# Sparse-attention weights scaled on GpSimd, values with v stationary, three branches summed in two PSUM banks

## The reference, cut to what matters

```
p_c = masked_softmax(q·kc - slope·dist)      # 15 compressed keys
o_c = p_c · vc
p_s = masked_softmax(q·ks - slope·dist)      # selected blocks: with 256 tokens all of them
o_s = p_s · vs
p_w = masked_softmax(q·kw - slope·dist)      # window of 512: the causal triangle
o_w = p_w · vw
masked_softmax: e = exp(s - max(s)); e / max(sum(e), 1e-30)
out = g0 * o_c + g1 * o_s + g2 * o_w         # g = sigmoid(gate_logits)
```

## Time and profile before

| | |
|---|---|
| median of 3 runs | 2322.37 us (2321.93 to 2323.93) |
| the profiled execution | 2321.79 us, span 2320.1 us |
| mean granted TensorE clock | 0.996 |
| TensorE busy | 2297.4 us, 99%, 13730 matmuls |
| VectorE busy | 1510.8 us, 65% |
| ScalarE busy | 1220.3 us, 53% |
| GpSimd busy | 63.2 us, 3%, 110 instructions |
| HBM read | 402.97 MB, 175 GB/s |

### The profile page before, as it was taken

How to read it: one execution, slowest core, us unless ns; L and a number is a source line. 1 busy time by engine, 2 the same in 40 slices (tenths; PEclk the granted TensorE clock), 3 DMA queues, 4 the chain that set the end, 5 groups by cost and what they waited for, 6 DMA issues and landing times.

```text
span 2320.1 us, 33059 instructions
## 1 busy us (share of the span) xinstructions
PE 2297.4 (99%) x13730; PEld 2003.9 (86%) x13730; DVE 1510.8 (65%) x2004; ACT 1220.3 (53%) x1813; POOL 63.2 (3%) x110
## 2 busy tenths in 40 slices
PE   8999999999999999999999999999999999999998
PEld 7888999988888889999888888888888988788887
DVE  5567656565665676565656765686777765785766
ACT  6555445464564554454545545454655554455554
POOL 0000000000000000000000100000000100000000
PEclk9999999999999999999999999999999999999999
DMA  8564543445545645434555434444555444445553
GB/s 287 189 212 181 204 146 128 167 179 190 192 175 188 212 180 204 146 128 166 214 191 191 164 145 153 151 151 163 208 182 182 164 146 164 145 163 181 183 189 109
DMA packets 61085, 406.69 MB, mean 175 GB/s; under 512 B 7784, under 2 KB 9320, under 8 KB 13576
## 3 DMA queue, kind: packets, MB, share of 16 engines
q1 hardware_dynamic: 60936, 404.58, 49.1%
HBM read 402.97 MB, written 2.10 MB: 175 GB/s over the span
## 4 chain that ended last, share of the span: by engine, by line
PE 94%; DVE 3%; ACT 2%; issue 1%; DMA 0%; SPq 0%; POOL 0%; DVEq 0%; POOLq 0%; ACTq 0%
PE bank L533 20%; PE bank L535 19%; PE bank L534 19%; PE bank L580 18%; PE bank L581 9%; DVE w_lo L249 1%; PE bank L1798 1%; PE bank L1658 1%; PE bank L2204 1%; PE bank L2230 0%; PE bank L396 0%; PE bank L2397 0%; PE bank L1961 0%; PE bank L1981 0%; PE bank L1971 0%
## 5 line engine op out<-in xcount | busy, mean ns | idle before, releaser
L249 DVE TENSOR_TENSOR w_lo<-w_raw,w_hi 128x2048 fp32r<-128x2048 f32 x368 | 837.9, 2284 | 84.0 <-ACT w_hi L241 83.7
L241 ACT ACTIVATE w_hi<-w_raw 128x2048 fp32r<-128x2048 f32 x368 | 702.3, 1911 | 126.3 <-DMA w_raw<-in_tiles 126.0
L580 PE MATMUL bank<-hT,w_hi 128*128 128x512 f32 x1920 | 680.6, 398 | 0.6 <-DVE w_lo L249 0.6
L581 PE MATMUL bank<-hT,w_lo 128*128 128x256 f32 x1920 | 539.0, 281 | 0.0
L580 PEld LDWEIGHTS bank<-hT,w_hi 128*128 128x128 f32 x1920 | 360.7, 188 | 89.6 <-DVE w_lo L249 1.4
L581 PEld LDWEIGHTS bank<-hT,w_lo 128*128 128x128 f32 x1920 | 362.6, 189 | 2.0
L533 PE MATMUL bank<-hT,w_hi 128*128 128x256 f32 x976 | 283.8, 291 | 0.0
L533 PE MATMUL bank<-w_hi,hT 128*128 128x512 f32 (+2 forms) x768 | 273.8, 357 | 5.6 <-DVE hT L385 5.6
L534 PE MATMUL bank<-hT,w_hi 128*128 128x256 f32 x976 | 278.1, 285 | 0.0
L535 PE MATMUL bank<-hT,w_lo 128*128 128x256 f32 x976 | 277.9, 285 | 0.0
L534 PE MATMUL bank<-w_lo,hT 128*128 128x512 f32 (+2 forms) x768 | 269.3, 351 | 0.0
(11 more groups left out here) (376 smaller groups left out, 3021.4 us busy)
## 6 DMA issues: line engine op xcount, KB each, us to landing
w_raw<-in_tiles SPq DMA_DIRECT2D x368, 1024.0 KB, 4.8
a_cmp_w<-in_cmp_w SPq DMA_DIRECT2D x2, 2048.0 KB, 7.7
w_raw<-in_tiles SPq DMA_DIRECT2D x8, 256.0 KB, 5.7
a_gm_rows<-in_rows SPq DMA_DIRECT2D x2, 768.0 KB, 6.5
x_res<-in_x SPq DMA_DIRECT2D x2, 512.0 KB, 5.8
a_ret_rows<-in_rows SPq DMA_DIRECT2D x2, 512.0 KB, 8.3
b_rows<-in_rows SPq DMA_DIRECT2D x2, 512.0 KB, 6.4
out<-x_res SPq DMA_DIRECT2D x4, 256.0 KB, 2.0
```

Source lines behind the costliest of these rows:

```text
L241: act.activation(k.hi[slot][:], k.raw[slot][:], ACT.Copy).then_inc(k.hi_done[slot], 1)
L249: dve.tensor_tensor(k.lo[slot][:], k.raw[slot][:], k.hi[slot][:].bitcast(F32), ALU.subtract).then_inc(k.lo_done[slot], 1)
L580: pe.matmul(bank[:], k.hi[slot][:, at:at + P], k.hT[:, c].rearrange("p a s -> p (a s)"), start=c == 0, stop=False)
L581: last = pe.matmul(bank[:, SEQ:2 * SEQ], k.lo[slot][:, at:at + P], k.hT_hi[:, c], start=False, stop=c == KC - 1)
```

## The change

1. Compressed attention: VectorE multiplies the weights by gate over sum before the turn (semaphore `scaled`), ahead of its filler work up to `cmp_pT`. `pT` becomes twice as large with zeros in half of it (a GpSimd memset), ScalarE copies into it in two halves of the partitions, and two products with `vd` stationary and 512 columns moving open banks 4 and 5, features in partitions.
2. Selected and window attention: a new `pool` program on GpSimd raises the sum to the power -1, multiplies by 1 + gate, and multiplies the two spans of the weights by it in place. The turn waits for that (`scaled`) instead of for the exponents.
3. Values: v stationary (64 columns), `pT` moving; all items add to what the compressed products left in banks 4 and 5. The heads are taken in the order 0, 5, 1, 4, ..., so that the two of a pair write different halves of the partitions. The values of a pair come an iteration later, behind the next pair's scores.
4. The filler units of an iteration stand together: 3, then 2 in each, then 1 and 3.
5. `weighted`, `y` and the turn of `y` go; ScalarE and VectorE split banks 4 and 5 directly, with the scale 0.5.
6. Grouped-query attention: the values of a pair come an iteration later too; filler units 2, 4, 4, 4, 2.

```diff
@@ Compressed @@
+        pool.wait_ge(self.part_mm, 2)
+        pool.memset(self.pT, 0.0).then_inc(self.pT_zeroed, 1)
...
-        f.vector(dve, "cmp_pT")
         dve.wait_ge(self.pr_ok, 1)
...
-        f.vector(dve, "cmp_pv")
-        for t in range(NT):
-            dve.wait_ge(self.pv_mm, t + 1)
-            last = dve.tensor_tensor(self.y[:, t]..., k.bank[4 + t]..., m[...], ALU.mult)
+        dve.tensor_tensor(self.pr[:], self.pr[:], m[:].unsqueeze(2).broadcast_to(wide), ALU.mult).then_inc(self.scaled, 1)
+        f.vector(dve, "cmp_pT")
...
-        act.activation(self.pT, self.k.bank[2][:], ACT.Copy).then_inc(self.pt_ok, 1)
+        act.wait_ge(self.pT_zeroed, 1)
+        for half in range(2):
+            r = slice(64 * half, 64 * half + 64)
+            last = act.activation(self.pT[r, :, half]..., self.k.bank[2][r, :]..., ACT.Copy)
+        last.then_inc(self.pt_ok, 1)
...
-        pe.wait_ge(self.pr_ok, 1)
+        pe.wait_ge(self.scaled, 1)
...
-        for a in range(4):
-            last = pe.matmul(k.bank[4 + a // 2][...], self.pT[:, a * P:(a + 1) * P], self.vd[:, a % 2, :], start=True, stop=True)
+        for g in range(2):
+            pe.matmul(k.bank[4 + g][:], self.vd[:, g], self.pT[:, g].rearrange("p f s -> p (f s)"), start=True, stop=False)
@@ Attention @@
-PAIRED = (0, 4, 1, 5, 2, 6, 3, 7)
+PAIRED = (0, 5, 1, 4, 2, 7, 3, 6)
...
         def turn_p(u):
-            pe.wait_ge(self.pr_ok, u + 1)
+            pe.wait_ge(self.scaled, u + 1)
...
+        def pv(p):
+            pe.wait_ge(self.pt_ok, 2 * p + 2)
+            for kc in range(2):
+                for u in (2 * p, 2 * p + 1):
+                    h, br = PAIRED[u % NSA_H], u // NSA_H
+                    d, c = P * br + 64 * (h // 4), h // 2
+                    out = k.bank[4 + c // 2][64 * (h % 2):64 * (h % 2) + 64, (c % 2) * SEQ + kc * P:(c % 2 + 1) * SEQ]
+                    keys = pT[u % 2][:, SEQ:SPAN] if kc else pT[u % 2][:, 0:SEQ]
+                    last = pe.matmul(out, self.vsvw[:, kc, d:d + 64], keys, start=False, stop=(...))
+            last.then_inc(self.pv_mm, 2)
...
         for p in range(U // 2):
-            f.tensor(pe, 1 if p else 2)
+            f.tensor(pe, 2 if p else 3)
             f.mark(f"nsa{p + 1}")
             for u in (2 * p + 2, 2 * p + 3):
                 if u < U:
                     qk(u)
+            if p:
+                pv(p - 1)
             for u in (2 * p, 2 * p + 1):
                 turn_p(u)
-            f.tensor(pe, 1)
-            for u in (2 * p, 2 * p + 1):
-                pv(u)
-        f.mark("nsa_o")
-        f.tensor(pe, 4)
+        f.tensor(pe, 1)
+        pv(U // 2 - 1)
         f.mark("nsa_y")
-        pe.wait_ge(self.y_ok, 2)
-        self.turn.tensor(pe)
+        f.tensor(pe, 3)
+
+    def pool(self, pool):
+        pool.wait_ge(*self.f.proj_out[self.f.n0 + 15])
+        factor = Link(pool, self.factors)
+        pool.memset(self.minus[:], -1.0)
+        factor(pool.tensor_scalar(self.gate1[:], self.gates[:], 1.0, None, ALU.add))
+        for u in range(self.U):
+            h, br, pr = PAIRED[u % NSA_H], u // NSA_H, self.pr[u % 2]
+            sm = self.sm[:, br, :, h:h + 1]
+            pool.wait_ge(self.pr_ok, u + 1)
+            factor(pool.tensor_tensor(sm, sm, self.minus[:].unsqueeze(2), ALU.pow))
+            factor(pool.tensor_tensor(sm, sm, self.gate1[:, :, 3 * h + 1 + br:3 * h + 2 + br], ALU.mult))
+            for a, b, t in self.spans:
+                last = pool.tensor_scalar(pr[:, a:b], pr[:, a:b], sm[:, t], None, ALU.mult)
+            last.then_inc(self.scaled, 1)
@@ Gqa @@
         for p in range(GQA_H // 2):
-            f.tensor(pe, 2)
+            f.tensor(pe, 4 if p else 2)
...
+            if p:
+                pv(p - 1)
             for u in (2 * p, 2 * p + 1):
                 turn_p(u)
-            f.tensor(pe, 2)
-            pv(p)
+        f.tensor(pe, 2)
+        pv(GQA_H // 2 - 1)
```

More of the change, by code:

```diff
@@ L1507, in vector @@
             rr = slice(32 * r, 32 * r + 32)
-            last = dve.tensor_copy(self.vd[rr, :, 64 * r:64 * r + 64],
+            last = dve.tensor_copy(self.vd[rr, :, 64 * (r % 2):64 * (r % 2) + 64],
                                    k.bank[5][rr, 0:P].rearrange("p (g d) -> p g d", g=2))
@@ L1556, in scalar @@
         act.wait_ge(self.pt_mm, 1)
-        act.activation(self.pT, self.k.bank[2][:], ACT.Copy).then_inc(self.pt_ok, 1)
+        act.wait_ge(self.pT_zeroed, 1)
+        for half in range(2):
+            r = slice(64 * half, 64 * half + 64)
+            last = act.activation(self.pT[r, :, half].rearrange("p g (t q) -> p g t q", t=NT),
+                                  self.k.bank[2][r, :].rearrange("p (t g q) -> p g t q", t=NT, g=2), ACT.Copy)
+        last.then_inc(self.pt_ok, 1)
     def tensor(self, pe):
@@ L1607, in tensor, with __init__ @@
         f.tensor(pe, 1)
-        f.mark("cmp_pv")
         pe.wait_ge(self.pt_ok, 1)
-        for a in range(4):
[L1611 to L1614, removed]
-PAIRED = (0, 4, 1, 5, 2, 6, 3, 7)
+        for g in range(2):
+            pe.matmul(k.bank[4 + g][:], self.vd[:, g], self.pT[:, g].rearrange("p f s -> p (f s)"), start=True, stop=False)
+PAIRED = (0, 5, 1, 4, 2, 7, 3, 6)
 class Attention:
     U = 2 * NSA_H
[L1626 to L1629, removed]
+    def __init__(self, k, ph, f, r, qT, kskwT, vsvw, gates, dist, split, before):
+        self.k, self.f, self.qT, self.kskwT, self.vsvw, self.gates, self.dist, self.before = (
+            k, f, qT, kskwT, vsvw, gates, dist, before)
+        self.y_hi, self.y_lo = split
         self.sc, self.pr, self.pT = ([r.at(f"nsa_{n}{j}", at + 1536 * j, [P, SPAN]) for j in range(2)]
@@ L1632, in __init__ @@
         self.nm, self.sm = r.at("nsa_nm", 38144, [P, self.U, NT]), r.at("nsa_sm", 38272, [P, 2, NT, NSA_H])
[L1633 to L1637, removed]
+        self.gate1, self.minus = r.at("nsa_gate1", 38400, [P, NT, 32]), r.at("nsa_minus", 38656, [P, NT])
+        (self.qk_mm, self.sc_ok, self.nm_ok, self.pr_ok, self.factors, self.scaled, self.pt_mm, self.pt_ok, self.pv_mm,
+         self.hi_ok, self.lo_ok) = (ph.sem("nsa_" + n) for n in (
+             "qk_mm", "sc_ok", "nm_ok", "pr_ok", "factors", "scaled", "pt_mm", "pt_ok", "pv_mm", "hi_ok", "lo_ok"))
         self.spans = ((0, P, 0), (P, SPAN, 1))
@@ L1660, in turn_p @@
             last.then_inc(self.pt_mm, 1)
[L1662 to L1675, removed]
+        def pv(p):
[6 more added lines that the diff above has]
+                    keys = pT[u % 2][:, SEQ:SPAN] if kc else pT[u % 2][:, 0:SEQ]
+                    last = pe.matmul(out, self.vsvw[:, kc, d:d + 64], keys, start=False, stop=(br == 1 and kc == 1 and h in (2, 3, 6, 7)))
+            last.then_inc(self.pv_mm, 2)
         f.tensor(pe, 1)
@@ L1719, in vector, with both @@
+    def both(self, y, n):
+        return y[:, 2 * n:2 * n + 2].rearrange("p c s -> p (c s)")
+    def vector(self, dve):
+        k, f, U, sc, nm = self.k, self.f, self.U, self.sc, self.nm
         for u in range(U):
@@ L1733, in vector @@
             last.then_inc(self.nm_ok, 1)
-        f.vector(dve, "nsa_o")
-        weighted(1)
         f.vector(dve, "nsa_y")
-        self.turn.vector(dve)
+        for n in range(2):
+            dve.wait_ge(self.hi_ok, n + 1)
+            dve.scalar_tensor_tensor(out=self.both(self.y_lo, n), in0=k.bank[4 + n][:], scalar=0.5,
+                                     in1=self.both(self.y_hi, n).bitcast(F32), op0=ALU.mult, op1=ALU.subtract
+                                     ).then_inc(self.lo_ok, 1)
     def scalar(self, act):
@@ L1766, in scalar @@
         f.scalar(act, "nsa_y")
-        self.turn.scalar(act)
+        self.k.ring.wait_used(act, *self.before)
+        act.wait_ge(self.pv_mm, U)
+        for n in range(2):
+            act.activation(self.both(self.y_hi, n), self.k.bank[4 + n][:], ACT.Copy, scale=0.5).then_inc(self.hi_ok, 1)
 class Fourier:
@@ L2556, in __init__ @@
         self.ret = Retention(k, ph, f, r, rqT, rkT, rv, rg, decay, ys[1], (self.gmlp.y_ok, NT))
-        self.cmp = Compressed(k, ph, f, r, nqT, kcvcT, gates, cbias, yn, self.gmlp, self.ret)
-        self.nsa = Attention(k, ph, f, r, nqT, kskwT, vsvw, gates, dist, yn, ys[0], f.last_use[0], self.cmp)
-        f.made = [(self.gmlp.lo_ok, 1), (self.ret.turn.lo_ok, YC), (self.nsa.turn.lo_ok, YC)]
-        self.out = Out(k, ph, f, mix_hi, mix_lo, (self.nsa.turn.lo_ok, YC))
+        self.cmp = Compressed(k, ph, f, r, nqT, kcvcT, gates, cbias, self.gmlp, self.ret)
+        self.nsa = Attention(k, ph, f, r, nqT, kskwT, vsvw, gates, dist, ys[0], f.last_use[0])
+        f.made = [(self.gmlp.lo_ok, 1), (self.ret.turn.lo_ok, YC), (self.nsa.lo_ok, 2)]
+        self.out = Out(k, ph, f, mix_hi, mix_lo, (self.nsa.lo_ok, 2))
         self.end, self.sum, self.add = self.out.end, self.out.sum, self.out.add
@@ L2602, in pool @@
         self.cmp.pool(pool)
+        self.nsa.pool(pool)
 class Middle2:
```

41 lines of the change are left out of this document (8 added, 33 removed).

## The result

The changed kernel takes 2352.57 us (median of 4 runs, 2349.22 to 2356.62), the kernel before beside it 2322.15 (2321.43 to 2323.93): a ratio of 1.013, 95% interval 1.0115 to 1.0145. The prediction said slower, 2333, with a range of 2315 to 2342. The direction was right, the size was not, and the range did not hold it.

A forecast was written before the change was run, and what follows sets the result against it. TensorE, 99% busy, was taken to bound the kernel. A gain of 7.6 us and 18.4 us of waits for GpSimd gave +10.8: 2321.8 to 2332.6, 2333 as median; own range 2324 to 2343, full range 2315 to 2342.

The forecast's parts named there:

- Gain on TensorE: Net work leaving TensorE: values 6.2, turn of y 1.7, grouped-query 0.3, less 0.6: 7.6 us, bounds 3 to 11.
- Values: Values of a pair on TensorE, from 1.34 us to 0.95: gain 6.2 us over 16 pairs, bounds 2.1 to 9.3.
- The compressed stage: VectorE's weighting is covered by filler, but a late combination holds the third filler unit 0.3 us a layer: cost 0.6.
- The place and the mechanism of the waits: GpSimd instructions begun inside w_lo end behind it; TensorE waits before turns in pairs 1, 4 and 7: 18.4 us.
- Rival 1: The port does not decide and GpSimd's start is not caught; only the 7.6 us gain is left: 2315, chance 0.20.
- the price of a unit: GpSimd's power, product and two multiplies (0.31 and 0.42) with signals: 1.9 us a unit, bounds 1.6 to 2.6.
- The third rival: GpSimd costs 2.6 us a unit and over, every pair near its due time, stalls 26 and more: 2341 or above, chance 0.10.
- rival 2: GpSimd is blocked once, but the multiplies slip ahead of the second w_lo: stalls 11.8 us, taken as 2325, chance 0.18.
- the two-stop picture: In pair 1 the first unit's power and the second unit's multiplies each stand behind a w_lo: TensorE stands 4.1 us.
- the clock behind the waits: The forecast sum has no term for TensorE running at a lower clock after its waits; it adds only 18.4 us of waits.
- the dearer unit: A GpSimd unit of 2.6 us instead of 1.9, for which stalls over two layers were put at about 26 us.

The follow-up runs named there:

- w_lo in four: Changed kernel with each w_lo subtraction of the selected and window attention cut into four of 512 columns: 2337.77 us, ratio 1.0076.
- filler as before: Changed kernel with the filler units of the kernel before (2, 2, ..., 2) instead of 3, 2, ..., 1: 2333.47 us, ratio 1.0051.
- an eighth: Changed kernel with GpSimd's two multiplies of a unit covering 16 and 32 columns instead of 128 and 256: 2325.09 us, ratio 1.0014.
- both: Changed kernel with two edits, the filler 2, 2, ..., 2 of the kernel before and w_lo in four parts: 2321.68 us, ratio 1.0002.
- one operand: Changed kernel with w_lo written by two half-tile VectorE multiplies by 1, reading one SBUF operand instead of two: 2316.95 us, ratio 0.9978.
- the run (2312.5 us): Changed kernel with GpSimd left at power and product, and the two long multiplies of a unit on VectorE ahead of the next w_lo: 2312.50 us.
- the unscaled kernel: Changed kernel without the GpSimd program of selected and window attention, the weights there left unscaled: 2312.01 us, ratio 0.9964.

## Why the prediction was right or wrong

**Gain on TensorE: right in kind, a little too small.** Predicted 7.6, measured 9.3 between medians and 10.0 by stages (9.0 and 1.0 of grouped-query attention). Values at 0.80 instead of the 0.95 that I took account for it (16 x 0.15 = 2.4). The compressed stage was right to the tenth: compressed scores to their turn 11.04 us against 10.74, 0.3 a layer.

**The place and the mechanism of the waits: right.** Pairs 1, 4 and 7, GpSimd's power begun just inside w_lo, a second stop in the second unit. Rival 1 (the port does not decide) is out.

**The miss, added up.** From 2333 to 2352.6 are 19.6 us. The waits were 26.8 instead of 18.4 (8.4 more). The slower clock behind them was not in the sum (11.8 more, worked out below). The gain was 2.4 larger. That makes 17.8; 1.8 us stay unassigned. With the waits alone mended the forecast would have stayed inside its range (2339); the clock took the result out of it. Two steps failed, then, and the larger one is a term put at nothing.

**The first step that failed: the price of a unit.** It is the one that reads "Taken as 0.31 and 0.42, a unit is 0.71 + 0.08 + 0.20 + 0.08 + 0.31 + 0.08 + 0.42 = 1.9 us". The two multiplies take 0.61 and 0.92, 1.51 together as printed, and a unit 2.6 us. The row I leaned on was the selection over 512 elements at 0.65: another instruction. The Trainium skill (GPSIMD Engine Reference, Engine selection) calls operations with one input roughly line rate against VectorE; here 1.51 us on GpSimd stand against 0.55 on VectorE for the same two, and the measurement decides. The true unit is at the upper end of my bounds (1.6 to 2.6), and the prediction itself gave stalls of about 26 for it. The third rival has this price, and its "2341 or above" holds the result, with a chance of only 0.10; but it expected idle time in all pairs, and it lay in three. By pair the waits in layer 0 were 4.9, 4.9 and 3.6 us, where I had 4.1, 2.6 and 2.5. For pair 4 I had taken the middle between a second stop (3.7) and none (1.5); the second stop came.

**For a unit of 1.9 us the 18.4 were too many.** With 1.77 us a unit 8.5 us were measured, because the second unit slips past w_lo. That is rival 2. Its 2325 is what this kernel took (2325.1), but that is luck: rival 2 had waits of 11.8 us, no slow clock and a smaller gain. So the two-stop picture was wrong for the unit that I assumed and right for the real one; 0.05 us decides between them.

**The second step that failed: the clock behind the waits, put at nothing without a reason.** Each of the three long waits of a layer is followed by 2.6 to 4 us of work at the lower level (in layer 0 from 365.09 to 368.71, 396.97 to 399.54 and 426.22 to 430.27). In the changed kernel 99 filler products at 0.21 instead of 0.12 are 8.9 us, and six groups of three turns at 0.87 to 0.90 instead of 0.40 are 2.9 more: 11.8. With the waits that makes 26.8 + 8.9 + 2.9 = 38.6 of the 40.0. The series of runs bears it out. Time above 2312.0 against the wait before the turns: 40.6 to 26.8 (changed), 25.8 to 17.4 (w_lo in four), 21.5 to 13.2 (filler as before), 13.1 to 8.5 (an eighth), 9.7 to 6.9 (both), 4.9 to 3.6 (one operand), 0.5 to 0. The time lost is 1.4 to 1.6 times the wait all along.

With the stall of 26 that the prediction gave for the dearer unit, the measured gain, and this factor of 1.5, which only the runs showed, the forecast would have been 2321.3 - 9.3 + 39 = 2351.

**Left open.** Whether the stop by itself, at an unchanged length of GpSimd and VectorE, carries more of the 40 us than the length: every run that weakened one touched the other's timing. Both are needed for the full loss: with short multiplies it is 13.1, with short stops 25.8.

## What to carry to other kernels

When work is moved to an idle engine, price it by a row of the same instruction on that engine, and ask what its neighbour on the shared port will be doing at the moment it starts; idle share says nothing about either. Elementwise scaling of a few hundred columns was free on a VectorE that was busy for 58% of the stretch, and cost 40 us on a GpSimd that was idle (21 with the filler order of before). Where TensorE is the bound, do not count a wait at its bare length: in the six kernels here that waited, the time lost was about one and a half times the wait. And put the link that TensorE waits for ahead of long work that can wait.

## What was not expected of the hardware

- GpSimd multiplies by a scalar per partition: 16 and 32 columns 0.67 us together, 128 columns 0.61, 256 columns 0.92 to 0.93. VectorE's two over 128 and 256 columns take 0.55 together.
- A stopped GpSimd instruction is let in at the end of each VectorE instruction (power 2.79 us behind one w_lo of 2.28, 1.19 behind w_lo in four parts), and VectorE instructions with one operand stop it too when they run at 0.63 ns an element.
- The granted clock was 0.67 and 0.86 in the stretches at and behind TensorE's wait of 4.2 us; between 340 and 430 it was 0.91 in the changed kernel and 1.00 in the run with one operand, whose longest wait was 1.1 us.
- VectorE stood for 1.7 us in pair 1 behind GpSimd, and the run (2312.5 us) shows no cost against the unscaled kernel (2312.0).
